# Mixing, MLP and gate stages of an encoder layer join one program block, with one memory map, weights split ahead and two norms applied behind the products

## The reference, cut to what matters

```python
hn = rms_norm(h, g_mix);  proj = hn @ w_in            # projection, q/k/v, rotary
od = diff_attention(...)                              # 4 heads, 512 columns
og = dilated_attention(...)                           # 8 heads; three patterns, mixed by softmax of lse
h = h + concat([od, og]) @ w_out                      # mixing
hn = rms_norm(h, g_mlp)
h = h + square(relu(hn @ w_up)) @ w_down              # MLP, 4096 wide
gate = sigmoid(rms_norm(h, g_ple) @ w_ple_gate)
h = h + gate * (p @ w_ple_proj)                       # gate
return rms_norm(h, g_final)
```

## Time and profile before

| | |
|---|---|
| three runs | 3502.57, 3508.45, 3509.76 us; median 3508.45 us |
| profiled execution | 3502.41 us, its span 3500.2 us |
| TensorE matmuls busy | 3294.4 us (94%), 18272 matmuls |
| VectorE / ScalarE / GpSimd busy | 1651.8 us (47%) / 1268.1 us (36%) / 818.9 us (23%) |
| mean granted TensorE clock | 0.981 |
| moved by DMA | 325.78 MB, mean 93 GB/s |

### The profile page before, as it was taken

One profiled execution on the slowest core, in us unless ns is written; L12 is line 12 of the kernel. 1 busy time (PEld: TensorE's weight loads), 2 busy tenths in 40 slices (PEclk: granted clock), 3 DMA queues, 4 the chain that ended last, 5 costly groups with the idle time before them and its releaser, 6 DMA issues. The chain is left out here.

```text
span 3500.2 us, 50866 instructions
## 1 busy us (share of the span) xinstructions
PE 3294.4 (94%) x18272; PEld 2827.8 (81%) x18272; DVE 1651.8 (47%) x2986; ACT 1268.1 (36%) x2302; POOL 818.9 (23%) x771
## 2 busy tenths in 40 slices
PE   8999998999999999939979999999999999996898
PEld 8988887888888899937758888888888888884787
DVE  5134445888888666634433333333433333333333
ACT  4011113777777688822231111111211111111332
POOL 2133330111111356502212222222222222221122
PEclk9999999999999999969989999999999999998999
DMA  5233337022303286445561111111511111114232
GB/s 180 75 107 121 122 122 170 20 54 52 80 20 81 67 184 156 116 136 188 185 222 49 49 49 50 49 50 50 162 51 49 48 48 48 48 36 151 83 116 83
DMA packets 253425, 325.78 MB, mean 93 GB/s; under 512 B 74448, under 2 KB 187728, under 8 KB 248016
## 3 DMA queue, kind: packets, MB, share of 16 engines
q1 hardware_dynamic: 249920, 317.38, 30.2%
q10 hardware_dynamic: 3344, 6.29, 0.7%
HBM read 230.95 MB, written 92.67 MB: 92 GB/s over the span
## 5 line engine op out<-in xcount | busy, mean ns | idle before, releaser
L1720 DVE TENSOR_TENSOR e_h<-e_down_acc,e_h 128x512 f32<-128x512 f32 x512 | 350.5, 691 | 847.6 <-PE e_down_acc L127 847.6
L125 PE MATMUL e_up_acc<-e_xt_hi,e_up_hi 128*128 128x512 f32 x1024 | 399.2, 390 | 20.8 <-DVE e_xt_lo L1697 20.8
L127 PE MATMUL e_up_acc<-e_xt_hi,e_up_lo 128*128 128x512 f32 x1024 | 398.8, 389 | 0.0
L126 PE MATMUL e_up_acc<-e_xt_lo,e_up_hi 128*128 128x512 f32 x1024 | 398.8, 389 | 0.0
L125 PE MATMUL e_down_acc<-e_down_hi,e_u_hi 128*128 128x512 f32 x1024 | 398.3, 389 | 0.0
L126 PE MATMUL e_down_acc<-e_down_lo,e_u_hi 128*128 128x512 f32 x1024 | 398.3, 389 | 0.0
L127 PE MATMUL e_down_acc<-e_down_hi,e_u_lo 128*128 128x512 f32 x1024 | 398.3, 389 | 0.0
L1740 POOL TENSOR_TENSOR e_sq<-e_r 128x512 f32<-128x512 f32 x128 | 133.8, 1045 | 1007.1 <-ACT e_r L1676 1007.1
L730 DVE TENSOR_REDUCE c_neg_half<-c_scores 128x1 f32<-128x1024 f32 x256 | 313.0, 1223 | 81.8 <-PE c_scores L815 81.7
L687 ACT ACTIVATE c_e<-c_scores,c_neg_max 128x1024 f32<-128x1024 f32 x256 | 287.1, 1121 | 58.8 <-DVE c_neg_max L737 50.8
L833 PE MATMUL c_pv<-c_v,c_at 128*128 128x128 f32 x2048 | 270.1, 275 | 0.4 <-ACT c_o L701 0.4
(11 more groups left out here) (161 smaller groups left out, 6694.3 us busy)
## 6 DMA issues: line engine op xcount, KB each, us to landing
s_qkt<-a_hl SPq DMA_DIRECT2D x128, 256.0 KB, 2.8
e_up_raw<-w_up_dram SPq DMA_DIRECT2D x32, 1024.0 KB, 5.7
e_down_raw<-w_down_dram SPq DMA_DIRECT2D x32, 1024.0 KB, 4.8
b_kt<-s_qkt SPq DMA_DIRECT2D x64, 256.0 KB, 9.4
a_w_raw<-w_in_dram SPq DMA_DIRECT2D x24, 512.0 KB, 5.3
d_nd<-s_nd SPq DMA_DIRECT2D x48, 256.0 KB, 4.1
b_qs<-s_qkt SPq DMA_DIRECT2D x32, 256.0 KB, 5.3
s_nd<-b_nout SPq DMA_DIRECT2D x16, 512.0 KB, 4.2
```

Of the source, the lines that this page charges most:

```text
L125: nc.tensor.matmul(out, lhs_hi, rhs_hi, start=first, stop=False)
L126: nc.tensor.matmul(out, lhs_hi, rhs_lo, start=False, stop=False)
L127: return nc.tensor.matmul(out, lhs_lo, rhs_hi, start=False, stop=last)
L1720: nc.vector.tensor_tensor(h[:, slot(z, t), cols], down_acc[:, k % 4], h[:, slot(z, t), cols], ALU.add).then_inc(S["h"], 1)
```

## The change

`Mix`, `Mlp` and `Gate` are now classes whose programs are appended to the one block of the first three stages; the barriers and clearings between stages are gone, and one clearing is left at the end. Seven things come with it.

1. A memory map: every tile has a written offset, so that tiles of a later stage lie where an earlier one is done, and waits for that are named (`wait_banks`, `wait_pattern1`, `wait_stored`, `wait_ups` and others). Semaphores of the first two stages are cleared by POOL inside the dilated stage (`finished`).
2. `w_out` is cut by rows into halves a and b. Half a is loaded in the dilated stage's head 1 and split by POOL in heads 2 to 5 (`split_a`); half b is loaded in head 6 and split by ACT and DVE at the start of mixing (`split_b`).
3. Mixing starts with the half of the product that needs only `od`: for tiles 0 and 1 chunks 0 to 3 come first, and the dilated half follows. The two halves of a turned tile have semaphores of their own.
4. The norm before the MLP moves behind the products: mixing turns `h` itself, DVE multiplies by `g_mlp` while copying out of PSUM (`h_out`), and `inverse` keeps 1/mean(h²) for each token. Since squared ReLU is quadratic, the MLP's additions into `e_h` become `down_acc * inv + h` (`scalar_tensor_tensor`).
5. `xt` of the first eight tiles is loaded back and split for the MLP during mixing's last eight tiles (`LATER`), and the first `up` weights are split in its last tile.
6. In the gate `g_ple` is multiplied into the weights while they are split, TensorE turns `h` itself, and the inverse root is the scale of the sigmoid. `h` is loaded once and serves as residual too.
7. Half a of the gate's weights is loaded in the MLP's second half and split between the last block's additions; half b and `w_ple_proj` are loaded when the last `up` product is done, and their `lo` parts are POOL's. Tile 0 is turned inside the last `down` products. The loops over tiles in mixing and gate are written out; the MLP's hardware loop stays.

The core of the diff:

```diff
+                        if h == HEADS - 1:
+                            store_md(p)
+                        if h == HEADS - 1 and p == 1:
+                            sp.wait_ge(S["scored"], h * WORK + 2 * PAIRS)
+                            mix.load_od(sp, 0)
+                            mix.load_od(sp, 1)
+                        if h == 1 and p == 1:
+                            mix.load_w(sp, 0)
+                        if h == HEADS - 2 and p == 1:
+                            sp.wait_ge(S["spread16"], 3 * (HEADS - 1))
+                            mix.load_w(sp, 1)
...
+                    if 2 <= h < 6:
+                        mix.split_a(pool, h - 2)
...
+            mlp.begin_tensor(pe)
+            dilated.wait_banks(pe)
+            turn(0, 0)
+            dilated.last_values(pe)
+            turn(1, 0)
+            for t in range(2):
+                for g in range(G):
+                    products(t, g, 0, KC // 2)
+            turn(0, 1)
+            for g in range(G):
+                products(0, g, KC // 2, KC)
+            turn(1, 1)
+            turn(2, 0)
+            for g in range(G):
+                products(1, g, KC // 2, KC)
+            turn(2, 1)
+            dilated.wait_results(pe)
+            self.turn_h(pe, 0)
+            for t in range(2, TILES):
+                if t + 1 < TILES:
+                    turn(t + 1, 0)
+                    turn(t + 1, 1)
+                for g in range(G):
+                    products(t, g, 0, KC)
+                self.turn_h(pe, t - 1)
...
+                if t + 2 < TILES:
+                    merge(t + 2)
+                if t >= TILES - LATER:
+                    mlp.split_xt_lo(dve, 0, t - TILES + LATER)
...
+                    nc.vector.scalar_tensor_tensor(out=tile, in0=self.down_acc[:, k % 4],
+                                                   scalar=self.fixed.inv[:, z * HT + t:z * HT + t + 1], in1=tile,
+                                                   op0=ALU.mult, op1=ALU.add).then_inc(S["h"], 1)
...
+                    if following is None and z + 1 == HALVES and k == 9:
+                        gate.turn(pe, 0)
```

More of the change, by code:

```diff
@@ L944, in used, with output, values @@
             return t if pattern(w) < 2 else t[:, :, :P]
+        def output(dve, w):
+            h, p = head(w), pattern(w)
+            dve.wait_ge(S["pv"], w + 1)
+            if w % PAIRS == 0 and h:
+                dve.wait_ge(stored[p], h * STORES[p])
+                dve.wait_ge(S["md"], NP * (h - 1) + p + 1)
+            t = w % PAIRS * 2
+            nc.vector.tensor_copy(nout[:, p, t:t + 2],
+                                  pv[:, w % 2, :2 * W1].rearrange("p (s x) -> p s x", s=2)).then_inc(S["out"], 1)
+        def values(pe, w):
+            h, p = head(w), pattern(w)
+            if w == 0:
+                differ.wait_results(pe)
+            if w % PAIRS == 0:
+                pe.wait_ge(v_in[p], (h // 2 + 1) * V_LOADS[p])
+            pe.wait_ge(S["et"], w + 1)
+            if w >= 2:
+                pe.wait_ge(S["out"], w - 1)
+            chunks, side = 2 if p < 2 else 1, h % 2 * W1
+            for s in range(2):
+                r, j = tile_of(w, s)
+                for c in range(chunks):
+                    ins = nc.tensor.matmul(pv[:, w % 2, s * W1:(s + 1) * W1], et[:, w % 2, s * chunks + c],
+                                           v[:, BASE[p] + r * CHUNKS[p] + j + c, side:side + W1],
+                                           start=(c == 0), stop=(c == chunks - 1))
+            ins.then_inc(S["pv"], 1)
         if True:
@@ L1223, in _ @@
                         score(w)
[L1224 to L1244, removed]
@@ L1554, in mlp_phase, with last_values, last_output, wait_stored @@
-def mlp_phase(kit):
-    nc, D = kit.nc, kit.dram
+                    if VALUES <= w < TOTAL + VALUES - 1:
+                        values(pe, w - VALUES)
+        def last_values(pe):
+            values(pe, TOTAL - 1)
+        def last_output(dve):
+            output(dve, TOTAL - 1)
+        def wait_stored(sp):
+            for p in range(NP):
+                sp.wait_ge(stored[p], STORES[p] * HEADS)
+            sp.wait_ge(md_stored, sum(STORES))
+        def wait_banks(pe):
+            pe.wait_ge(S["masked"], 2 * TOTAL)
@@ new lines, in slot, with blocks, begin_scalar, begin_vector @@
+    def slot(self, z, t):
+        return (z * self.HT + t) % self.H_SLOTS
+    def blocks(self, eng, step):
+        FB = self.FB
+        for z in range(self.HALVES):
+            step(z, 0, z * FB, 1)
+            with eng.Fori(1, FB - 1) as f:
+                step(z, f, f + z * FB, f + 1)
+            step(z, FB - 1, z * FB + FB - 1, None)
+    def begin_scalar(self, act):
+        for name in "xt_hi up_hi down_hi relu u_hi".split():
+            act.sem_inc(self.S[name], START)
+    def begin_vector(self, dve):
+        for name in "xt_lo up_lo down_lo h".split():
+            dve.sem_inc(self.S[name], START)
@@ L2086, in build @@
     nc.all_engine_barrier()
-    nc.clear_and_free_semaphores(kit.sems)
+    for name in "dilated mix mlp gate".split():
+        nc.clear_and_free_semaphores(kits[name].sems)
     nc.all_engine_barrier()
-    for phase in PHASES:
-        kit = Kit(nc, dram)
-        phase(kit)
-        nc.all_engine_barrier()
-        nc.clear_and_free_semaphores(kit.sems)
-        nc.all_engine_barrier()
 def shape_constants():
```

1642 lines of the change are left out of this document (882 added, 760 removed).

## The result

The changed kernel took 3549.92 us (median of 4 runs, 3545.92 to 3555.26), the kernel before 3507.65 us beside it (4 runs, 3502.57 to 3509.76). The ratio is 1.0124, 95% interval [1.0105, 1.0143]: the changed kernel is 42 us (1.2%) slower, where the prediction had a gain of 112. The profiled execution took 3547.25 us, its span 3545.2 us.

A forecast was written before the change was run, and what follows sets the result against it. TensorE was taken as the bound, with matmuls in flight for 94% of the span, leaving three hand-overs to shorten. 40 + 4 + 24 + 43.5 - 3 = 108.5 off 3502.4 gave 3393.9, stated as 3396 us; range 3377 to 3418.

The forecast's parts named there:

- the gate's 16 tiles took 240.2 us: Gate tiles: writing out the loop gains nothing, since 15.0 us a tile of TensorE work gives 240.3 us.
- my slower case: Rival, MLP: its additions become DVE-bound, from 1.43 us each; at 1.5 it adds 144 us, 3538 us; chance 0.03.
- my signs of being wrong: Wrong if the waits for `d_mixed` behind tile 2 sum to over 30 us, or the MLP's 1395 us grow.
- The clock: Start of mixing: new waits may bring spells of matmuls at half pace; 3 us of loss (0 to 6).
- The rest of mixing: From tile 2's products to mixing's last: 191 us instead of 194.9, 9 us of it waits; gain 4, bounds 0 and 12.
- my chain: Mixing, each tile: residual, `h_out`, store, issues, landing, merge and POOL take 14.9 us; TensorE needs the tile after 14.7.
- The rival in which mixing stays bound by its loads: Mixing: first loads late, each later tile waits as before or more; gain 86, 3416 to 3422 us; chance 0.12.
- POOL beside DVE: Mixing's last eight tiles: DVE's `e_xt_lo` subtraction of 1.3 us may delay POOL's additions in six tiles, 8 us in all.
- Start of mixing: First load at 1504, tile 0 turned at 1517, tile 2's products at 1545 instead of 1585.2; gain 40, bounds 29 and 48.
- The trap at tile 3: Start of mixing: tile 3's load stands behind tile 0's store of `h`; tile 2's products wait some 8 us.
- MLP and both hand-overs: Into the MLP 2 × 1.03 us instead of 26.2, gain 24; its additions cost 0; into the gate, gain 43.5.
- The gate's hand-over: From MLP to gate: 3.7 us instead of 47.2, 0.9 of it a wait; gain 43.5, bounds 34 and 44.4.

The follow-up runs named there:

- e1: Changed kernel with the gate's embedding of tile t+2 requested ahead of the store of tile t, instead of t+1: 3408.56 us, ratio 0.971.
- e5: Kernel before, with the gate's embedding requested for the next tile, behind the store of the tile before, instead of the one after: 3679.26 us, one run.
- e3: e1 plus, in mixing, values and `od` of tile t+3 requested where those of t+2 were: 3370.7 us, ratio 0.9606.
- e8: Changed kernel with the reload of `xt` moved behind the requests for the next tile's values: 3539.12 us, ratio 1.0092.
- e2: Changed kernel with only mixing's requests of values and `od` made a tile earlier, gate's queue unaltered: 3511.25 us, ratio 1.0009.
- e4: Changed kernel with DVE's splits of `e_xt` in mixing moved behind the residual and `h_out`: 3544.09 us, one run.
- e9: e8 plus the edit of e4, against the changed kernel: 3533.4 us, ratio 1.0077.
- e7: Kernel before with unused tiles behind the small tiles, so that operands begin at multiples of 64 bytes: 3510.07 us, ratio 1.0007.

## Why the prediction was wrong

**The step that failed** is "the gate's 16 tiles took 240.2 us, and 60 × 0.227 + 10 × 0.14 is 15.0 a tile ... its hardware loop cost nothing, so nothing is gained". I counted TensorE's work in those tiles and took the loads as hidden, as they were in the kernel before. In the changed kernel TensorE waited 111.5 us there for the embedding, and the tiles took 374.6 us. The loops were rewritten, and with them SP's queue; nowhere did I follow that queue through a tile of the gate, as I had done for mixing. The line `if t and t + 1 < TILES: self.load_emb(sp, t + 1)` ahead of the store of t, and so behind the store of t-1, was to be read before the run. It cost 134 us against the old tiles (e1, e5), and no rival had it: my slower case was in the MLP, where nothing happened. Nor did my signs of being wrong: the waits for `d_mixed` behind tile 2 sum to 23.4 us and the MLP took 1395.1, so neither of the two showed. That the count gave 240.3 for 240.2 us was luck. The gate's matmuls started every 0.2325 us, not every 0.227, and ten turned blocks cost some 1.0 us a tile, not 1.4 (e1: 234.1/16 - 60 × 0.227); the two errors cancelled.

**The clock** was priced at 3 us. The spells at 0.50 cost 29.0 us in the gate (e1) and 187.56 - 176 = 12 in mixing (e3), because the waits came in every tile or every second one, and the long ones are followed by such a spell.

**The rest of mixing**: the mechanism was right and the size was off. The two effects were named (one load more for SP, DVE's split beside POOL) and the chain was called on the edge, but "I take 9 us for all waits" should have been 23.4 (211.0 - 187.56), plus the 12 us of slow matmuls. The landing of 3.9 us in my chain was that of one tile, and the median of the kernel before was 4.3. "Issues 1.8" was the old figure too; in the changed kernel the three requests of values alone took 1.9 to 3.9 us, for a cause that stays open. The load more was priced at its issue of 0.5 us; moving it was worth 9 to 11 us (e8). With the values requested a step earlier no wait is left (e2, e3), though the requests still stand behind the stores of the tile before: they have a tile's time to spare. The rival in which mixing stays bound by its loads had the right place, with 7 us lost in this stretch where 16.1 were.

**POOL beside DVE**: foreseen from tile 8 on, at 1.3 us a tile; measured 0.9 us longer additions in six tiles, 5.5 us, of which 2 to 6 reach the time (e4, e9). The rule of the Trainium skill, page "SBUF — State Buffer", section "Who interferes with whom", agrees with the trace: an addition of 1.29 us that begins 0.15 us behind a 1.22 us subtraction with two SBUF inputs takes 2.18 us. It loses 0.9 of the 1.07 us for which the subtraction still ran.

**Start of mixing**: 33.8 of 40 us. The first load was issued at 1509.36, not 1504. The last store of sums alone takes 2.27 us to issue (1504.99), and `od` landed late ahead of the last dilated product. Tile 0 was turned at 1522.4, not 1517. The trap at tile 3 was there, as forecast at 8 us, in two parts: 3.28 us for `od` of tile 3 and 4.67 us for its `d_mixed`. (In its working 1532.5 and the four terms give 1544.6, not 1544.3, and the upper bound for the rest of mixing, 194.9 - 182, is 13, not 12; nothing hangs on either.)

```profile
1538.42 0.32 SPq L1409 DMA_DIRECT2D s_h<-d_h  x1
1538.79 1.77 SPq L1397 DMA_DIRECT2D d_nd<-s_nd  x3
```

The values themselves were requested 0.4 us behind that store.

**MLP and both hand-overs** were right. The MLP starts 0.7 us behind mixing's last product (24 us forecast, 25.5 got), `up` and `down` never wait, and the additions with their scalar operand are hidden, at 749 ns on average against 691:

```profile
L1883 DVE SCALAR_TENSOR_TENSOR e_h<-e_down_acc,g_inv,e_h 128x512 f32<-128x512 f32 x512 | 378.2, 749 | 815.4 <-PE e_down_acc L140 815.1
```

The gate's hand-over gave 46.2 us for 43.5; its only wait is 0.2 us for `f_w_lo`. With SP's requests made a tile earlier, in the gate and in mixing, the kernel is 25 to 31 us under the forecast: 3370.7 and 3365.5 us against 3396. Some 9 us of that are the matmuls' faster pace, which I had not foreseen, and another 9 the waits in mixing that no longer come.

## What to carry to other kernels

When a change rewrites a loop, follow every queue through one period of it, also where the stage had no wait before: a request that needs nothing, behind a store that needs everything, can be hidden when it is for the tile after the next, and costs a wait in every tile when it is for the next one (in the gate here none, and 8 us). Where such a wait recurs, add what the matmuls behind it lose to the clock, here another quarter (29.0 of 111.5 us in the gate) to a half (12 of 23.4 in mixing) of the waits themselves. An early reload for a later stage is not free for the present one: put it behind the loads that the present chain waits for.

## What the runs showed of the hardware that was not expected

Behind a pause of 7.8 us the granted clock stood at 0.50 (1.2 GHz) over the next 2.8 us of matmuls. In mixing it was 0.50 in the 3.0 us behind a wait of 4.93 us, and 0.69 and 1.00 behind two waits of 2.1 us:

```profile
1580.30:1583.30 3.00, 2.95 (x15) 2.52 (x16) 1.38 (x2) 0.74 (x2) 0.00 (x0) 1.00 1.03 394
1595.30:1598.30 3.00, 2.96 (x11) 2.42 (x12) 1.38 (x2) 0.73 (x2) 0.00 (x0) 0.69 0.99 379
1659.50:1662.50 3.00, 2.98 (x9) 2.56 (x10) 1.52 (x3) 0.93 (x2) 0.00 (x0) 0.50 0.96 317
```

In the earlier trace rows only the three long holes between stages and the tail show a mean clock well under 1.00.

The same product with the same shapes ran at 397 ns a matmul and one per 0.2325 us in the old mixing and gate stages, and at 390 ns and one per 0.227 us in the changed kernel and in every MLP. It is not the clock (1.00 in both) and not alignment to 64 bytes (e7). The old gate's last two tiles, which lie outside its hardware loop, have the slower pace too. What sets it was not found.
